# Final norm of the next tile made inside VectorE's wait, and one ring of weights that runs through all three phases

## What is computed

```
hf = rmsnorm(x, norm_ffn_g[l])
x = x + peer_ffn(hf, ...)          # per token 128 rows of peer_u, and of peer_v
return rmsnorm(x, final_g)         # the final norm of the first block

def hybrid_layer(x, w_in, w_out, ln_g, ln_b, rel_bias, topk):     # run twice
    proj = x @ w_in                # qA kA vA gA, qB kB vB gB, index qI kI wI
    oA = stick_breaking_attention(qA, kA, vA)
    oB = dsa_sparse_attention(qB, kB, vB, qI, kI, wI, rel_bias, topk)
    mix = concat([oA * silu(gA), oB * silu(gB)])
    return layer_norm(ALPHA * x + mix @ w_out, ln_g, ln_b)
```

## Time and profile before

| what | value |
|---|---|
| median of 3 runs | 2979.33 us (2976.88 to 2986.76) |
| the profiled execution: its time | 2977.58 us |
| its span, from the first to the last instruction | 2975.8 us |
| group 0, first DMA to first DMA of the next | 1601.2 to 2155.4 us |
| group 1 | 2155.4 to 2655.5 us |
| group 2 | 2655.5 us to the end |
| PE busy | 81% of the span |
| DVE busy | 59% |
| DMA, mean over the span | 271 GB/s |

### The profile page before, as it was taken

One profiled execution on the slowest core, in us unless ns is written; L12 is line 12 of the kernel. 1 busy time (PEld: TensorE's weight loads), 2 busy tenths in 40 slices (PEclk: granted clock), 3 DMA queues, 4 the chain that ended last, 5 costly groups with the idle time before them and its releaser, 6 DMA issues. The chain is left out here.

```text
span 2975.8 us, 30375 instructions
## 1 busy us (share of the span) xinstructions
PE 2398.3 (81%) x9779; PEld 1605.8 (54%) x9779; DVE 1751.3 (59%) x3656; ACT 908.0 (31%) x1740; POOL 987.2 (33%) x691
## 2 busy tenths in 40 slices
PE   6997999869878898898786986797566467559897
PEld 4776878758663343343333664575345336337575
DVE  3444311032136988988975688587759869755151
ACT  4444222233322222222222443243133324323232
POOL 2332555343232343344342234234323523310001
PEclk9998999989998999999898997899678678759898
DMA  4321333223139899999999899899799999964553
GB/s 158 97 67 50 98 98 101 81 81 126 49 121 347 314 406 415 416 409 402 395 410 405 333 379 372 314 371 394 295 355 384 416 409 398 380 260 172 216 190 140
DMA packets 257323, 805.56 MB, mean 271 GB/s; under 512 B 18366, under 2 KB 139862, under 8 KB 191655
## 3 DMA queue, kind: packets, MB, share of 16 engines
q0 software_dynamic: 73728, 536.90, 44.8%
q1 hardware_dynamic: 183463, 267.06, 25.6%
HBM read 795.07 MB, written 14.07 MB: 272 GB/s over the span
## 5 line engine op out<-in xcount | busy, mean ns | idle before, releaser
L1337 POOL DMA_INDIRECT gathered<-in_peer_rows,experts x436 | 532.5, 1221 | 918.2 <-DVE x_res L2635 607.0
L1695 PE MATMUL peer_banks<-gathered,peer_diags 128*128 128x512 f32 x720 | 338.3, 626 | 56.2 <-ACT peer_diags L1750 56.2
L78 PE MATMUL group_banks<-group_x_t,group_ring 128*128 128x128 f32 (+1 forms) x2016 | 338.1, 331 | 16.7 <-ACT group_x_t L2447 8.4
L2621 DVE CUSTOM_DVE_ANT_0 gathered<-gathered,late_nat 128x1024 f32<-128x1024 f32 x256 | 317.8, 1244 | 35.0 <-DMA gathered<-in_peer_rows,experts 29.9
L2635 DVE SCALAR_TENSOR_TENSOR x_res<-gathered,group_weights,x_res 128x1024 f32<-128x1024 f32 x256 | 331.4, 1295 | 2.7 <-DVE group_weights L2627 0.3
L78 PEld LDWEIGHTS group_banks<-group_x_t,group_ring 128*128 128x128 f32 x2016 | 305.4, 207 | 46.3 <-ACT group_x_t L2447 10.8
L1695 PEld LDWEIGHTS peer_banks<-gathered,peer_diags 128*128 128x128 f32 x720 | 142.2, 201 | 241.7 <-issue 241.7
L2261 PE MATMUL group_banks<-group_ring,group_x_t 128*128 128x512 f32 x512 | 233.7, 611 | 28.4 <-DMA group_ring<-in_weights 28.4
L1790 DVE CUSTOM_DVE_ANT_0 peer_product<-gathered,early_nat 128x1024 f32<-128x1024 f32 x180 | 214.7, 1222 | 37.9 <-DMA gathered<-in_peer_rows,experts 36.6
L1695 PE MATMUL peer_banks<-early_gathered,peer_diags 128*128 128x512 f32 x304 | 149.3, 643 | 51.7 <-ACT peer_diags L1750 51.7
L2261 PEld LDWEIGHTS group_banks<-group_ring,group_x_t 128*128 128x128 f32 x512 | 98.3, 197 | 150.2 <-issue 117.0
(11 more groups left out here) (376 smaller groups left out, 4201.6 us busy)
## 6 DMA issues: line engine op xcount, KB each, us to landing
group_ring<-in_weights SPq DMA_DIRECT2D x270, 512.0 KB, 4.7
mixer_wq<-in_w_in SPq DMA_DIRECT2D x24, 512.0 KB, 4.1
mixer_wk<-in_w_in SPq DMA_DIRECT2D x24, 512.0 KB, 4.1
peer_w<-in_w_pq SPq DMA_DIRECT2D x8, 1024.0 KB
gathered<-in_peer_rows,experts POOLq DMA_INDIRECT x436
diff_wv<-in_w_in SPq DMA_DIRECT2D x8, 512.0 KB, 4.0
conv_wb<-in_w_in SPq DMA_DIRECT2D x8, 512.0 KB, 4.0
merge_w<-in_w_conv_out SPq DMA_DIRECT2D x8, 512.0 KB
```

Of the source, the lines that this page charges most:

```text
L78: last = nc.tensor.matmul(out, lhsT, rhs, start=n == 0, stop=n == len(pairs) - 1)
L1337: nc.gpsimd.indirect_dma_start(row_buffer(m, r), None, A["peer_rows"], bass.IndirectOffsetOnAxis(ap=at, axis=0))\
L1695: last = nc.tensor.matmul(ps[:, ACC[unit % 2] + half, :], diags[:, r % DIAGS, :], row_buffer(m, r)[:, D + half * BANK:D + (half + 1) * BAN ...
L2621: nc.vector.tensor_tensor_reduce(out=row, in0=row, in1=m.late_nat[:, t % 2, :], scale=1.0, scalar=0.0, op0=ALU.mult, op1=ALU.add, accum_ou ...
```

## The change

1. **Final norm of the next tile in this phase.** In a phase that has a next one (`keeps`), ACT's `next_roots` and DVE's `scale_next` do the final norm of the next tile ahead of `inverse_roots` and `add_output` of the last layer. SP loads `final_g` into `mix[:, 0, :]`, whose content has been turned by then; the squares go to `work`. Groups 1 and 2 start without a norm (`SCALES` is 0), and their PE transposes at once. Group 0 starts as before.
2. **The rows end one point earlier.** The last `("norm")` point has weight 0, so that all 133 steps are done by `("out")` of the last layer. The other points get more: by that layer's last point ahead of `gated_sparse` there are 126 steps in group 0 (124 before) and 127 in group 1 (125 before); in layer 0 it is one more at the same place in either group.
3. **One ring.** Ring and semaphores are made once (`m.ring`, `m.w_loaded`). At the end of a phase SP goes on with the next phase's first six blocks (kI, qI 0 to 3, v0 0) as the `out` blocks are used. Group 2's values lie in the memory of `gathered`, which is not needed there.
4. **Order on SP.** What stood behind the load that follows `out` 3 stands behind the load that follows `out` 0: the last store of keys, and in layer 0 the bias tiles, old index keys and old values of layer 1. `affine` of layer 0 waits for nothing in groups 1 and 2.

```diff
+        points[-1] = (points[-1][0], 0)
...
-        ring = sb("ring", [P, WS, D])
+        ring = m.ring
...
-                    l, b = divmod(n, BLOCKS)
-                    sp.dma_start(ring[:, n % WS, :], A["weights_2"][l, b]).then_inc(w_loaded[n % WS], 16)
+                    l, b = divmod(n % (LAYERS * BLOCKS), BLOCKS)
+                    place = (FIRST_BLOCK + n) % WS
+                    sp.dma_start(ring[:, place, :], A["weights_2"][l, b]).then_inc(w_loaded[place], 16)
...
                 for n in range(WS, LAYERS * BLOCKS + WS):
-                    if n < LAYERS * BLOCKS:
+                    if n < LAYERS * BLOCKS or keeps:
                         load_block(n)
...
-                    if b == WEIGHTS.index(("out", 3)):
+                    if b == WEIGHTS.index(("out", 0)):
                         if keeps:
                             store_keys(l, UNITS - 1)
+                        if l + 1 == LAYERS and keeps:
+                            sp.wait_ge(proj_done, job_at[l, "mix1", last] + 1)
+                            sp.dma_start(next_gain, A["final_g"].unsqueeze(0).to_broadcast([P, D])).then_inc(next_gain_loaded, 16)
                         if l + 1 < LAYERS:
                             load_bias(l + 1, 0)
...
+                    if l + SCALES:
+                        pe.wait_ge(normed, 2 * NT * (l - 1 + SCALES) + 2 * (t - first) + n + 1)
...
+                def next_roots():
+
+                    act.wait_ge(m.row_added, bg.first + bg.rows)
+                    act.wait_ge(attended, UNITS * LAYERS)
+                    for n, t in enumerate(next_tiles):
+                        nc.scalar.activation(junk, m.x[:, t, :], ACT.Square, accum_out=next_total[:, n:n + 1]).then_inc(next_squared, 1)
+                    act.wait_ge(next_var_ready, len(next_tiles))
+                    nc.scalar.activation(next_var[:, :], next_var[:, :], ACT.Ln).then_inc(next_inv_step, 1)
+                    act.wait_ge(next_inv_step, 1)
+                    nc.scalar.activation(next_inv[:, :], next_var[:, :], ACT.Exp, scale=-0.5).then_inc(next_inv_ready, 1)
...
                     done = gelus((l, "out"), done)
-                    inverse_roots(l + 1)
+                    if l + 1 == LAYERS and keeps:
+                        next_roots()
+                    inverse_roots(l + SCALES)
...
+                def scale_next():
+
+                    for n in range(len(next_tiles)):
+                        dve.wait_ge(next_squared, n + 1)
+                        nc.vector.tensor_scalar(next_var[:, n:n + 1], next_total[:, n:n + 1], 1.0 / D, 1e-6, ALU.mult, ALU.add).then_inc(next_var_ready, 1)
+                    dve.wait_ge(next_inv_ready, 1)
+                    dve.wait_ge(next_gain_loaded, 16)
+                    for n, t in enumerate(next_tiles):
+                        nc.vector.scalar_tensor_tensor(out=m.x[:, t, :], in0=m.x[:, t, :], scalar=next_inv[:, n:n + 1], in1=next_gain,
+                                                       op0=ALU.mult, op1=ALU.mult).then_inc(next_scaled, 1)
...
                     done = rows((l, "out"), done)
+                    if l + 1 == LAYERS and keeps:
+                        scale_next()
                     add_output(l)
```

More of the change, by code:

```diff
@@ L1977, in group_stage @@
     bg = Background(next_tiles, tiles)
-    WS = 6
+    WS, FIRST_BLOCK = RING, number * LAYERS * BLOCKS
+    SCALES = 0 if number else 1
     UNITS = 2 * PAIRS
@@ L2003, in group_stage @@
         q_t, k_t = sb("q_t", [P, 2, NQ]), sb("k_t", [P, 3, (last + 1) * P])
-        values = [sb(f"values{half}", [P, last + 1, HALF]) for half in range(2)]
+        if keeps:
+            values = [sb(f"values{half}", [P, last + 1, HALF]) for half in range(2)]
+        else:
+            values = [m.gathered[:, half, :].rearrange("p (t n) -> p t n", n=HALF) for half in range(2)]
         work = sb("work", [P, 3, 2, SC])
@@ L2014, in group_stage @@
         var, log_var, inv = sb("var", [P, NT]), sb("log_var", [P, NT]), sb("inv", [P, NT])
+        next_total, next_var, next_inv = (sb(n, [P, len(next_tiles)]) if keeps else None for n in ("next_total", "next_var", "next_inv"))
+        junk, next_gain = work[:, :, :, :].rearrange("p n e c -> p (n e c)")[:, 0:D], mix[:, 0, :]
         if bg.rows:
@@ L2017, in group_stage @@
         rel = [work[:, 2, :, :].rearrange("p e c -> p (e c)"), share[:, :, :].rearrange("p t c -> p (t c)")]
-        w_loaded = [sem(f"w_loaded{n}") for n in range(WS)]
+        w_loaded = m.w_loaded
+        next_gain_loaded, next_squared, next_var_ready = sem("next_gain_loaded"), sem("next_squared"), sem("next_var_ready")
+        next_inv_step, next_inv_ready, next_scaled = sem("next_inv_step"), sem("next_inv_ready"), sem("next_scaled")
         head_w_loaded, affine_loaded, stored = sem("head_w_loaded"), sem("affine_loaded"), sem("stored")
@@ L2110, in pairs_of @@
                                 store_keys(l, u - 1)
-                for n in range(2):
-                    load_block(n)
-                sp.dma_start(affine[:, 0, :], A["final_g"].unsqueeze(0).to_broadcast([P, D])).then_inc(affine_loaded, 16)
+                if number == 0:
+                    for n in range(2):
+                        load_block(n)
+                    sp.dma_start(affine[:, 0, :], A["final_g"].unsqueeze(0).to_broadcast([P, D])).then_inc(affine_loaded, 16)
                 sp.dma_start(head_w[:, :, :, :], A["head_weights_2"]).then_inc(head_w_loaded, 16)
@@ L2120, in _ @@
                     load_old_values(0, SPARSE)
-                for n in range(2, WS):
-                    load_block(n)
+                if number == 0:
+                    for n in range(2, WS):
+                        load_block(n)
                 load_bias(0, 0)
@@ L2546, in copy_mix @@
                             .then_inc(proj_copied, 1)
+                def next_roots():
[7 more added lines that the diff above has]
+                    nc.scalar.activation(next_inv[:, :], next_var[:, :], ACT.Exp, scale=-0.5).then_inc(next_inv_ready, 1)
                 done = 0
                 nc.scalar.preload_act_table_set("natural_log_exp_and_others")
-                for n, t in enumerate(tiles):
-                    made = nc.scalar.activation(mix[:, n, :], m.x[:, t, :], ACT.Square, accum_out=inv[:, n:n + 1])
-                    made.then_inc(squared, 1)
-                done = gelus((0, "first"), done)
-                inverse_roots(0)
+                if SCALES:
+                    for n, t in enumerate(tiles):
+                        nc.scalar.activation(mix[:, n, :], m.x[:, t, :], ACT.Square, accum_out=inv[:, n:n + 1]).then_inc(squared, 1)
+                    done = gelus((0, "first"), done)
+                    inverse_roots(0)
                 for l in range(LAYERS):
@@ L2792, in _ @@
                 done = rows((0, "first"), done)
-                scale_input()
+                if SCALES:
+                    scale_input()
                 each = DSA_TOPK // 8 // PAIRS
@@ L2947, in program @@
                 peer_stage(nc, A, m, h_t, nat)
-            for number in range(len(GROUPS) - 1):
+            m.ring = buffer(experts, "ring", [P, RING, D])
+            m.w_loaded = [nc.alloc_semaphore(f"w_loaded{n}") for n in range(RING)]
+            for number in range(len(GROUPS)):
                 group_stage(nc, A, m, number, out)
-        group_stage(nc, A, m, len(GROUPS) - 1, out)
 def laid_out(inputs):
```

18 lines of the change are left out of this document (8 added, 10 removed).

## The result

The changed kernel takes **2990.75 us** (median of 12 runs, 2983.33 to 2999.38) against 2978.61 of the kernel before (12 runs, 2970.96 to 2990.41): ratio **1.0034, 95% interval 1.0018 to 1.0050**, slower. The forecast was 2960 with a range of 2942 to 2973. The profiled execution of the changed kernel took 2985.57 us, its span is 2983.8.

What follows compares the result with a forecast made beforehand. DMA was taken as nearly full in group 1, with a jam at its start next to free time. Terms -8.7 - 23 + 5 + 5 + 3.5 = -18 us took 2977.6 to 2959.4 profiled, so 2960 us, range 2942 to 2973.

Steps and rivals of the forecast that it cites:

- Term 1: Group 1 to group 2: adds and norm leave the stretch from normalise to first projection, -8.7 us (bounds -11.3 and -7.5).
- Term 2: Group 0 to group 1, up to the index scores: earlier start and no wait for v0's blocks, -23 us.
- Term 3: Rest of group 1 behind the index scores: DMA takes back part of the lead, +5 us.
- Term 4: Change of layer: SP's 1.97 MB for layer 1 ahead of `out` 7 delay the output, +5 us.
- Term 5: Groups 0 and 1: two more background steps ahead of `gated_sparse` by layer 1's end, +3.5 us, bounds 0 and 10.
- `final_g` did land late: End of groups 0 and 1: DVE waits for the late load ahead of `add_output`, slower, 2994; chance 0.04.
- DMA takes the lead back: Group 1's end comes from bytes, gathers and SP's order cost their full price, 2970; chance 0.16.

Runs made afterwards that it cites:

- the ring alone: Kernel before with only the ring of weights carried over between phases; final norm at each phase's start, rows and SP's order as before: 2955.45 us, 0.9915.
- both costs undone: Changed kernel with SP's loads of layer 1 back behind the last output block and rows spread as before up to the last `gated_sparse`: 2950.51 us, 0.9901.
- The gelus later: The 2950.51 us kernel (SP's order and rows as before) with ACT's first gelus in groups 1 and 2 behind the input's copies: 2949.50 us, 0.9896.
- the rows back: Changed kernel with SP's order as changed, but rows spread as before up to the last `gated_sparse`, last adds ahead of the final norm: 2976.94 us, 0.9993.

## Why the prediction was wrong

- **Term 1**, -8.7 us: right. 14.86 us became 5.80, so -9.1. The moved work was hidden; `add_output` waited for PE's product, not for the scaling.
- **Term 2**, -23 us: right. Last mix of group 0 to the index scores of group 1 went from 105.9 to 82.4 us, -23.5. The scores come 35.3 us behind the transposes, and no block is waited for over 2 us. With the ring alone it is 87.6 us, so most of the term is the ring's.
- **Term 3**, +5 us: not contradicted, but its size isn't shown. With both costs undone, the stretch behind the scores is 3.5 us longer, 174.8 against 171.3; the same stretch took 171.0 to 174.3 us in the runs with order, bias or values moved on the kernel before, in which nothing inside this stretch was changed. The gelus later show the kind of the term: a lead of 11 us taken back with 14.
- **Term 4**, +5 us with bounds 0 to 11.7 in group 1 and 0 in group 0: **the first step that failed**, 27 us alone, 16 in the changed kernel. The three outputs grew by 5.8, 15.9 and 1.8 us. Two things were wrong in it. The upper price was bytes by 168 GB/s, "beside gathers"; but the 39 us of the earlier trace rows hold 6 in which SP had DMA nearly for itself, and 30 at 108 GB/s. By 108 the 1.97 MB take an estimated 18 us. And the share depends on the packets: bias moves in short ones and gets 9% of the bytes in group 0 (above) and 18% in group 1 (0.38 of 2.07 MB from 2396 to 2401 us in the changed kernel), where 168 of 411 GB/s are 41%. And "gathers stop there, since DVE waits too" took the traffic for gone: DVE's last add in group 1 ended at 2398.8, but gathers already issued kept their turns until 2412. `out` 7 landed 20.1 us behind its issue, in group 0, too, 18.0 us.
- **Term 5**, +3.5 us with bounds 0 to 10: **the second step**, 18 us alone, 14 in the changed kernel. It priced two steps by DVE's own time, 5.1 us, and put the waits for ACT's gelus at nothing. In layer 1 of group 0 those waits are the cost: 29.3 us in the changed kernel against 8.5 with the rows back, where the stretch from v0 to the last mix takes 207.0 against 189.1 us and DVE works 151.4 against 150.7. In layer 0 of group 1 the rows cost 6 to 7 us more (183.5 against 177.4, 181.8 against 174.8); DMA is 0.99 to 1.00 busy in the latter two, and whether the added step costs its time on DVE or its transfer stays open there. In layer 1 of group 1, from v0 on, they cost nothing (225.3 us with them, 225.2 and 225.4 without).
- The sum of terms 1 to 3, with both others at nothing, is -26.7: measured -30.
- **Rivals.** `final_g` did land late (DVE waited 9.16 us for it in group 0, 2.55 in group 1), but PE came later still, by 6.70 and 4.07 us; this was not what made the kernel slower. "DMA takes the lead back" had the right resource for the order. It priced order and gathers at 10 us together in group 1, again too little. No rival had the order itself as the mechanism of a slower kernel.

## What to carry to other kernels

A load's share beside gathers is its packets' size, not its bytes: price a load that is moved ahead of an awaited one by its own packets, and take the transfers already in flight as still ahead. Read such a rate from a stretch in which both queues have work all the time. Background work that is moved costs more than its own time: it moves every wait for its helpers, here ACT's gelus, so leave its spread alone and move only the last pieces. Two good changes (here 30 us) can be hidden by two lines that came with them, so time the parts alone.

## What was not expected of the hardware

The equality of packets was closer than thought: 582 to 577, 266 to 261, 145 to 146 in stretches of 4 to 11 us, and 1254 to 1247 in 30 us. A block of 0.5 MB landed 1.28 us behind the one before it once the gathers were through, and 3.77 us behind it beside them (SP's blocks in the kernel before, group 1).
